# DeltaNet solve interleaved with attention, attention's output by way of DRAM, and the last three matrix stages run without a barrier

## What is computed

```
h      = rms_norm(x) * (1 + scale) + shift              # scale, shift, gate from silu(cond) @ w_mod
proj   = h @ w_in                                       # 1024 -> 9008, feeds three mixers and three gates
a      = gated DeltaNet over q, k, v, both directions, chunks; needs the inverse of
         (I + strictly lower part of beta * k k^T * decay) for each block of tokens and head
o_a    = rms_norm(o_fwd + o_bwd) * silu(z_a)            # branch_a = o_a @ w_branch_a
o_b    = softmax(q k^T) v * silu(z_b)                   # 8 heads, 2 key heads; branch_b = o_b @ w_branch_b
y      = rms_norm((ssd_fwd + ssd_bwd + d * x) * silu(z_c))   # branch_c = y @ w_branch_c
merged = sigmoid(g_a) * branch_a + sigmoid(g_b) * branch_b + sigmoid(g_c) * branch_c
x      = x + gate * (merged @ w_out)
```

## Time and profile before

| what | value |
|---|---|
| median of 3 runs | 5306.74 us (5296.28 to 5310.59) |
| the profiled execution's own time | 5286.49 us |
| its span, first to last instruction | 5284.8 us |
| TensorE busy with matmuls | 4230.5 us, 80% |
| VectorE / ScalarE / GpSimd busy | 2144.9 us (41%) / 1033.5 us (20%) / 634.1 us (12%) |
| mean granted TensorE clock | 0.875 of full |
| moved by DMA | 495 MB, mean 94 GB/s |

### The profile page before, as it was taken

The page is one execution under the profiler, slowest core; times in us unless marked ns, Lnnn a source line. Parts: engine busy times, 40 slices in busy tenths (PEclk is TensorE's granted clock), DMA queues, the critical chain, the costliest instruction groups (busy, mean ns, idle before and its releaser), DMA issues.

```text
span 5284.8 us, 65448 instructions
## 1 busy us (share of the span) xinstructions
PE 4230.5 (80%) x25101; PEld 3952.1 (75%) x25101; DVE 2144.9 (41%) x2634; ACT 1033.5 (20%) x1805; POOL 634.1 (12%) x700
## 2 busy tenths in 40 slices
PE   5899999967771865898769999996978538649977
PEld 2899999955761864887739999996848528648867
DVE  2532521067435346444235134112563353464442
ACT  2111100041211211342021011000611212124410
POOL 0000010015120002000000000001161200030000
PEclk8999999989785877998879999998988768769988
DMA  6222222123245431002252222221242634210024
GB/s 215 100 83 76 90 96 85 64 91 131 86 133 165 130 96 58 10 6 78 83 170 88 87 80 90 92 89 47 92 147 80 190 109 148 81 31 9 6 83 150
DMA packets 424230, 494.97 MB, mean 94 GB/s; under 512 B 86179, under 2 KB 360325, under 8 KB 416461
## 3 DMA queue, kind: packets, MB, share of 16 engines
q1 hardware_dynamic: 386472, 393.05, 23.4%
q0 software_dynamic: 32848, 98.24, 4.9%
q10 hardware_dynamic: 4700, 0.88, 0.1%
HBM read 334.51 MB, written 157.57 MB: 93 GB/s over the span
## 4 chain that ended last, share of the span: by engine, by line
PE 69%; DMA 9%; DVE 9%; issue 4%; SPq 3%; POOL 3%; ACT 2%; DVEq 1%; POOLq 0%; ACTq 0%
PE PSUM L642 15%; PE PSUM L644 15%; PE PSUM L643 15%; PE PSUM L1289 5%; PE PSUM L1136 4%; PE PSUM L1310 3%; DMA g_XY<-xy_d 1%; PE PSUM L1278 1%; SPq L835 1%; PE PSUM L1009 1%; PE PSUM L1008 1%; DMA w_mod<-in_w_mod 1%; PE PSUM L1279 1%; POOL x_in L1718 1%; PE PSUM L1094 1%
## 5 line engine op out<-in xcount | busy, mean ns | idle before, releaser
L642 PE MATMUL PSUM<-h_hi,w_hi 128*128 128x384 f32 x3456 | 1156.3, 335 | 40.1 <-DVE w_lo L628 40.1
L643 PE MATMUL PSUM<-h_lo,w_hi 128*128 128x384 f32 x3456 | 1155.9, 334 | 0.0
L644 PE MATMUL PSUM<-h_hi,w_lo 128*128 128x384 f32 x3456 | 1155.8, 334 | 0.0
L642 PEld LDWEIGHTS PSUM<-h_hi,w_hi 128*128 128x128 f32 x3456 | 650.1, 188 | 40.3 <-issue 40.3
L643 PEld LDWEIGHTS PSUM<-h_lo,w_hi 128*128 128x128 f32 x3456 | 650.0, 188 | 0.0
L644 PEld LDWEIGHTS PSUM<-h_hi,w_lo 128*128 128x128 f32 x3456 | 649.9, 188 | 0.0
L642 PE MATMUL PSUM<-b_hi,w_hi 128*128 128x384 f32 x1152 | 394.5, 342 | 112.9 <-DVE w_lo L628 55.4
L626 DVE CAST w_hi<-w_raw 128x2048 fp32r<-128x2048 f32 (+1 forms) x104 | 118.9, 1144 | 796.9 <-PE PSUM L644 587.1
L643 PE MATMUL PSUM<-b_lo,w_hi 128*128 128x384 f32 x1152 | 391.7, 340 | 0.0
L644 PE MATMUL PSUM<-b_hi,w_lo 128*128 128x384 f32 x1152 | 391.5, 340 | 0.0
L642 PEld LDWEIGHTS PSUM<-b_hi,w_hi 128*128 128x128 f32 x1152 | 222.1, 193 | 118.1 <-issue 109.3
(11 more groups left out here) (307 smaller groups left out, 6290.8 us busy)
## 6 DMA issues: line engine op xcount, KB each, us to landing
w_raw<-in_w_in SPq DMA_DIRECT2D x70, 1024.0 KB, 5.0
proj_d<-leave POOLq DMA_DIRECT2D x140, 512.0 KB, 3.0
g_t<-gdn_tile_d SPq DMA_DIRECT2D x36, 1024.0 KB, 8.6
gdn_tile_d<-g_out SPq DMA_DIRECT2D x18, 1792.0 KB, 7.2
wide<-proj_d SPq DMA_DIRECT2D x48, 576.0 KB, 3.8
w_mod<-in_w_mod SPq DMA_DIRECT2D x12, 2048.0 KB, 18.3
xs<-ssm_tok_d SPq DMA_DIRECT2D x36, 640.0 KB, 5.0
qk_t<-proj_d SPq DMA_DIRECT2D x36, 512.0 KB, 10.0
```

What stands on the lines that cost most here:

```text
L642: pe.matmul(dst, wh, x_hi[:, k, lo:hi], start=(k == 0), stop=False)
L643: pe.matmul(dst, wh, x_lo[:, k, lo:hi], start=False, stop=False)
L644: last = pe.matmul(dst, wl, x_hi[:, k, lo:hi], start=False, stop=(k == kt - 1))
```

## The change

The order of the stages becomes: 3 DeltaNet preparation, 4 attention preparation, 5 attention with the solve in it, 6 SSD preparation, 7 SSD scan, 8 gating of the SSD output, 9 its branch, 10 DeltaNet scan, 11 gating, 12 DeltaNet branch, 13 attention's branch, 14 output projection. In detail:

- VectorE's solve is cut into 62 slots, one in each head of attention. ScalarE's four flips stand in the first four heads of the last (short) tile. SP stores the result after the last tile's output, ahead of the barrier. SP loads the blocks ahead of the first tile of attention preparation.
- Attention's output is stored to DRAM by tile (`obz_d`) and not split into `b_hi` and `b_lo`. It is loaded back at the start of the gating of the DeltaNet output, ahead of the gate tiles, and split in four blocks during the DeltaNet branch.
- In DeltaNet preparation ScalarE's queue issues the loads of `gin`, GpSimd's queue issues the stores of the diagonal blocks of the second direction, one tile late.
- `XY`, `T` and the new `T6` are cleared at the start of the scan stage, by VectorE and GpSimd; the inverse loads wait for it. `T6` and `Y6` are formed by products of whole 128x128 tiles.
- No engine waits between stages 12, 13 and 14 (`arrive` in place of `barrier`). The first group of the output projection is multiplied in two halves: the first four blocks of `merged`, then the rest. `merged` is split block by block as it is finished.
- Some semaphores are shared, which changes their counts.

```diff
+        obz_d = dram("obz_d", [4, P, T])
...
+        def blocks_out(e, t, d):
+            for c in range(4):
+                at = slice(c * SOLVE, (c + 1) * SOLVE)
+                src = g_out[t % 2][at, 6 * d].rearrange("p (h t) -> p h t", t=P)[:, :, at]
...
+                e.dma_start(dst.rearrange("h (j i) -> j h i", i=SOLVE), src).then_inc((g_pstored if d else g_stored)[t % 2], 16)
...
 # SP
+                def ob_store(t, p):
+                    sp.wait_ge(gated, nth(l, t, 0, 3) + 1)
+                    sp.dma_start(obz_d[:, :, cols(t)].rearrange("k p t -> p k t"), o_bz[p][:]).then_inc(ob_out[p], 16)
+                zb_load(0)
+                for t in range(NT):
+                    ob_store(t, t % 2)
+                    if t < NS:
+                        zb_load(t + 1)
+                sp.wait_ge(xy_done, l * 4 + 4)
+                for d in range(2):
+                    sp.dma_start(xy_d[d], xy_out[:, d]).then_inc(xy_stored, 16)
+                    for h in range(GH):
+                        sp.dma_start(xy_p_d[d, h::4], xy_out[32 * d + 4 * h:32 * d + 4 * h + 4, 2]).then_inc(xy_stored, 16)
+                for p in range(2):
+                    sp.wait_ge(ob_out[p], (l + 1) * (5 - p) * 16)
+                barrier(sp, l, 5)
...
                 tile_loads(0)
                 tile_loads(1)
-                sp.wait_ge(xy_done, l * 4 + 4)
...
+                sp.wait_ge(g_clear, l * 4 + 4)
                 sp.wait_ge(xy_stored, l * 160 + 160)
                 inverse_loads(0)
                 inverse_loads(1)
...
+                sp.dma_start(ob_raw[:], obz_d.rearrange("k p t -> p k t")).then_inc(ob_in, 16)
+                z_loads(z_a, B_ZA, 4, 2)
+                barrier(sp, l, 11)
                 branch(G_GDN, "w_branch_a", 4, B_GATE)
-                barrier(sp, l, 10)
+                arrive(sp, l, 12)
                 branch(G_ATT, "w_branch_b", 4, B_GATE + 8)
                 arrive(sp, l, 13)
                 branch(G_OUT, "w_out", 8, None)
...
 # TensorE
+                def t_six(t):
...
+                        products(d, 4 * d + 3, operand(t, d, K_A), lambda h: x[:, h])
+                def y_six(t):
...
+                        products(d, 4 * d + 1, lambda h: gd[d]["T6"][:, h], lambda h: y[:, h])
...
+                early, late = range(0, 4), range(4, KT)
+                for j in range(4):
...
+                    if j == 0:
+                        pe.wait_ge(m_lo, l * KT + 4)
+                    for b in range(2):
+                        pe.wait_ge(acc_free[b], l * NG + n + 1)
+                        out_part(p, b, early, True)
+                        if j:
+                            out_part(p, b, late, False).then_inc(acc_ready[b], 1)
+                    if j == 0:
+                        pe.wait_ge(m_lo, l * KT + KT)
+                        for b in range(2):
+                            out_part(p, b, late, False).then_inc(acc_ready[b], 1)
...
 # ScalarE, attention
+                        if nk == 1 and h < 4:
+                            flip_inverse(h)
...
-                    act.wait_ge(gated, nth(l, t, 2, 3) + 1)
-                    act.activation(b_hi[:, 0:4, cols(t)], o_bz[:], ACT.Copy).then_inc(hi_made, 1)
...
 # VectorE, attention
                         elif nk > 1:
                             head_max(t + 1, 1 - u, 0)
+                        solve_slot(t * AH + h)
                         dve.wait_ge(at_t[0], n * AH + h + 1)
...
+                    elif i < 8 or 54 <= i < 58:      # a product and an update
+                        m = 35 - i if i < 8 else 58 - i
+                        solve_product(m)
+                        solve_update(m)
+                    elif i < 54:                     # one of the two
...
 # VectorE, branches
+                branch(G_GDN, 4, merge_more, lead=split_att)
+                arrive(dve, l, 12)
+                branch(G_ATT, 4, merge_last, lead=lambda: split_group(dve, l, G_OUT, 0, G_OUT // 2, KT))
+                arrive(dve, l, 13)
+                branch(G_OUT, 8, merge_out, begun=split_late)
```

More of the change, by code:

```diff
@@ new lines, in out_part @@
+                def out_part(p, b, ks, first):
+                    for c in range(3):
+                        lo, hi = c * THIRD, (c + 1) * THIRD
+                        dst = bank(3 * b + c, THIRD)
+                        for j, kk in enumerate(ks):
+                            wh = w_hi[p][:, kk, b * P:b * P + P]
+                            wl = w_lo[p][:, kk, b * P:b * P + P]
+                            pe.matmul(dst, wh, b_hi[:, kk, lo:hi], start=(first and j == 0), stop=False)
+                            pe.matmul(dst, wh, b_lo[:, kk, lo:hi], start=False, stop=False)
+                            last = pe.matmul(dst, wl, b_hi[:, kk, lo:hi], start=False, stop=(not first and j == len(ks) - 1))
+                    return last
```

1087 lines of the change are left out of this document (558 added, 529 removed).

## The result

The changed kernel takes 5073.4 us (median of 4 runs, 5068.4 to 5088.2), the kernel before 5304.2 us on the same measure; the ratio is 0.957, with a 95% interval of 0.955 to 0.959. That is 231 us less, where the prediction had 170 less: the time lies under the range that was given (5085 to 5197 us). The profiled execution takes 5068.4 us, its span 5066.6 us.

What follows compares the result with a forecast made beforehand. TensorE was taken to wait on inverse-block loads (mainly the solves), split weights, the merged sum's split and exponentials. Terms of -85 us per layer, -170 in all, took the 5306.7 us median to 5137 us; range 5085 to 5197.

Steps and rivals of the forecast that it cites:

- Step 1: Head of the DeltaNet scan: solve leaves the path, scan's own loads remain; 87 to 23 us, -64 us per layer.
- Step 2: Solve slots inside attention's heads: fit in 2.0 us of VectorE slack per head, cost 0 to 1 us per layer.
- Step 3: Attention's edges: copy gone -12, flips +7, stores of the inverse +9, together +4 us; block loads before it +3 us.
- Step 4: DeltaNet preparation: clearing moved -4 us, input loads and block stores on other queues -1 us; -5 us per layer.
- Step 5: DeltaNet scan: full T6 and Y6 products take 1.95 us, not 1.71, per 16 records; +1 us per layer.
- my signs of being wrong: Attention taking over 330 us per layer, or the head of the scan taking over 40 us.
- Step 6: Gating of the DeltaNet output: 2.4 MB of attention's output loaded ahead of the gate tiles; +5 us per layer.
- Step 7: Three last matrix stages run on without barriers: 38 us of waiting and slow clock become 8; -30 us per layer.
- (a): Rival: the solve's slots lie on attention's path and both solves come back whole; 5259 us, 9%.
- (b): Rival: the last branches save nothing, weight loads staying behind gate loads in SP's queue; 5197 us, 7%.
- (c): Rival: loads at the scan's head and the small stores cost their upper ends; 5191 us, 12%.
- (d): Rival: slots leave TensorE gaps in attention's heads and its clock falls to 0.50; 5664 us, 2%.

## Why the prediction was wrong, point by point

The direction, the largest term and the mechanism of what the change was meant to do were right; the sum was 64 us short of the gain. In the profiled executions the miss is 48 us (218 against 170), and the rest is the step from one execution to the median.

**Step 1, head of the scan, right.** -65.0 and -64.8 for -64; the head is 22 us of loads, near the 23 that the slices of the old profile gave. (At 7.65 MB in 24 us the 3.5 MB come to 11 us and not 10, so the sum should have said 24.)

**Step 2, the slots, right.** VectorE's turn in a head is as drawn, and TensorE's waits for the copy come to 3.8 us in both layers. The rule of the Trainium skill (SBUF — State Buffer, section SBUF: two separate sides) stayed without effect: the longest product of the solve is 0.96 us as before. That neither confirms nor denies it, since the casts of the queries at the tile changes mostly lay beside the row maximum, which reads PSUM; one product in each layer overlapped a cast, by some 0.1 us.

**Step 3, attention's edges, right within 3 us in the profiles compared** (+6.5 for +5 with the slots), as a sum of errors of opposite sign: stores 7 for 9; the waits for exponentials gave 16 us in two layers and not 24. It is in part luck: over all profiles attention takes 326 us in the old order and 322 us in the new one with its stores as in the change, -4 for +5 (see the median, below).

**Step 4, DeltaNet preparation, the term mis-sized.** -5 became -11.8. I read the DMA share of 1.02 as "another queue moves nothing faster". Two runs show 3.1 and 3.6 us for the two moves, where I had 1 us for both. The share was 1.02 over 15 us, but 0.75 over the whole stage of the old profile: I took the full stretch for the stage. That the queues cost their time between such stretches, where a load was issued behind eight stores, fits this and wasn't looked at further.

**Step 5, T6 and Y6, the step that failed.** Its term was +1 us for the scan; the scan gave -13.5 and -19.8 us, -13.8 in the mean of the new order. I priced the products by their own duration, +0.5 us a tile, and took TensorE's wait as a cover that only hides costs. But the quarter products cost their neighbours: the 32 records behind them took 5.29 to 6.07 us in twelve of 18 tiles, and 3.74 us behind full products in all 18. The price of 1.95 against 1.71 us was right and beside the point. In the old trace this could be seen: clock 0.86 in a stage that is busy for 184 of 213 us. I didn't ask why, and none of my signs of being wrong looked at the scan. That the full products are worth 5 us alone and 11.5 us together with the address is shown in the old order; why quarter products let the clock fall in some tiles and not in others is open. The page TensorE: Matmul & The Clock Gate of the Trainium skill (section HAM oscillation — how this bites in real kernels) describes the other half, a wait for a DMA in every tile that leaves the next products slow, and the trace agrees in part: behind full products, waits of 3.8 and 4.2 us left the next group at 2.97 and 3.65 us, one of 2.65 us left it at 2.02. But the length of the wait doesn't settle it alone: in the same scan of the changed kernel waits of 3.25 and 3.54 us left the next group at 2.02 us, and with the weights early one of 2.52 us left it at 3.63.

**A part that I never costed: the address.** The tile that became permanent stood in the diff as a line without a price. By the runs it is worth 11.5 - 5 = 6 to 7 us per layer in the scan once the products are full, and 29 us of the kernel before with full products (5293.4 to 5264.2 us). Moved to 32 of 256, the changed kernel is 44 us slower; the scan is 27 of them, against its mean. Of the other 17 SSD preparation could hold some, with 144.3 and 140.8 us where the profile of the changed kernel has 133.0 and 142.5, but it varies as much without any edit. Shown is that address and landing go together. Why they do is only argued: the page DMA: Bandwidth & Descriptors of the Trainium skill (section How a descriptor splits into AXI transactions) says that each transaction has to start at a multiple of 256 bytes, so a piece that doesn't start there is split from the multiple below it. By an estimate from that account the 512-byte pieces of a query and key tile would touch 3, 3 and 2 blocks of 256 at offsets 96, 128 and 0, and they landed in 10.0, 9.8 and 9.1 us in the old order; in the new one it is 9.7 us at 32 (3 blocks) and 8.8 at 0. That fits 9.1, but not 9.8 below 10.0. The page gives its account for reads; here it is writes to SBUF.

**Step 6, gating, right** (+4.5 for +5).

**Step 7, the last three stages, mis-sized.** -21.6 for -30. The wait ahead of the output projection is 8.3 us and not 3: I saw that SP comes late with the weights but not that VectorE's merges, and so TensorE's accumulators, stand behind their splitting. The run with the weights early took both waits to under 1 us and gave more than I had lost there.

**The stages not touched** gave 9.7 and 5.6 us. Their code is the same, and SSD preparation alone ranges from 132.6 to 145.3 us over all runs, with a mean of 140.7 us in the old order and 139.5 us in the new one; I leave that as spread.

**From the profile to the median.** I added the 20 us by which the profile of before lies under its median. After, that is 5 us. Seven profiles of kernels in the old order have attention at 318 us in seven layers and at 326.6 to 338.8 us in seven; in the new order no layer is above 326.8. The profile of before had 318.5 twice, a kind draw. So the old attention stage is on average 326 us, and the change took away some of that too. That it is the wait of 1.73 us at each tile change which brings the slow layers is my guess; it was not tried.

Of the rivals, (a), (b) and (c) would each have ended at 5191 us or more, and what they rest on was not seen; (d) didn't come: the clock in attention is 0.93 over the stage and 0.97 up to 1590 us, ahead of the last, short tile with the flips and stores.

## What to carry to other kernels

Price a product by what it does to the clock of its neighbours, and not by its own record: where a stage's granted clock is low although TensorE is nearly always busy, look for reduced products and for the wait they fall into. In this scan the wait hid two things, slow products and late loads, and taking away either showed 5 us or nothing while both together gave 11.5. Read the diff also for what moves addresses: a small tile that becomes permanent shifts every buffer behind it, and can cost as much as an edit that was meant gains.

## What I had not expected of the hardware

Idle time on TensorE can be worth less than useless work: twelve products per tile that nobody reads, 2.75 us each time, made the kernel 27 us faster, 15 of them in the scan, and 24 of them made it neither faster nor slower. With the scan's buffers at 0 rather than 96 modulo 256 bytes the 512 KB loads of its queries and keys landed in 8.8 to 9.1 us rather than 10.0 us. And the same stage with the same code took 318 us in one layer and 336 us in another of the same execution: two layers of one profile are two draws, and one profile is a thin base for a median.
